# One decoder layer on one core: norm factors per token in partitions, both residual steps on VectorE through PSUM, and a tail in groups of chunks

## The reference

```python
x = x + 0.5 * rmsnorm(swiglu(rmsnorm(x, g1_pre), gate1, up1, down1), g1_post)     # D_FF 5632
p = rmsnorm(x, g_mix_pre) @ w_in              # q k v o | conv a b | input and forget gates
mix = concat[mlstm(q, k, v, gates) * sigmoid(o), silu(layernorm(conv31(a * sigmoid(b))))]
x = x + rmsnorm(mix @ w_out, g_mix_post)
x = x + 0.5 * rmsnorm(swiglu(rmsnorm(x, g2_pre), gate2, up2, down2), g2_post)
# rmsnorm(x, g) = x * rsqrt(mean(x*x) + 1e-6) * g
```

## Time and profile before

| what | us |
|---|---|
| median of three runs (lowest, highest) | 2255.87 (2255.12, 2260.18) |
| the profiled execution, its own time | 2259.16 |
| span of the profiled execution | 2257.5 |
| TensorE busy | 2202.1 |
| VectorE, ScalarE, GpSimd busy | 1008.4, 893.8, 1097.4 |

### The profile page before, as it was taken

How to read it: one execution, slowest core, us unless ns; L and a number is a source line. 1 busy time by engine, 2 the same in 40 slices (tenths; PEclk the granted TensorE clock), 3 DMA queues, 4 the chain that set the end, 5 groups by cost and what they waited for, 6 DMA issues and landing times. The chain is left out here.

```text
span 2257.5 us, 42395 instructions
## 1 busy us (share of the span) xinstructions
PE 2202.1 (98%) x16454; PEld 2183.2 (97%) x16454; DVE 1008.4 (45%) x1329; ACT 893.8 (40%) x1138; POOL 1097.4 (49%) x635
## 2 busy tenths in 40 slices
PE   8999999999999998999999998999999999999995
PEld 8999999999999998899999998999999999999995
DVE  7533332233333227867757716633332223334324
ACT  5433333333333334444344535433333333333331
POOL 4444443344444446656657576444444334444444
PEclk9999999999999999999999999999999999999998
DMA  5545555545545543445645453445445445454452
GB/s 213 163 164 166 166 168 166 163 157 167 167 164 165 169 163 117 165 171 195 219 162 205 150 177 117 150 167 165 163 161 171 165 161 168 164 163 158 168 166 88
DMA packets 100312, 371.20 MB, mean 164 GB/s; under 512 B 11120, under 2 KB 13296, under 8 KB 99216
## 3 DMA queue, kind: packets, MB, share of 16 engines
q1 hardware_dynamic: 96192, 349.93, 46.6%
q10 hardware_dynamic: 3920, 20.18, 2.5%
q0 software_dynamic: 128, 0.07, 0.0%
HBM read 357.06 MB, written 13.07 MB: 164 GB/s over the span
## 5 line engine op out<-in xcount | busy, mean ns | idle before, releaser
L1466 POOL TENSOR_TENSOR wlo<-raw,whi 128x1024 fp32r<-128x1024 f32 x369 | 892.8, 2421 | 827.9 <-ACT whi L736 816.2
L382 PE MATMUL bank<-xh,whi 128*128 128x288 f32 x3600 | 1079.3, 300 | 19.8 <-DVE xl L1040 19.6
L383 PE MATMUL bank<-xl,whi 128*128 128x288 f32 x3600 | 1066.2, 296 | 0.0
L384 PE MATMUL bank<-xh,wlo 128*128 128x288 f32 x3600 | 1065.7, 296 | 0.0
L736 ACT ACTIVATE whi<-raw 128x1024 fp32r<-128x1024 f32 x658 | 694.5, 1057 | 654.5 <-PE bank L384 639.2
L1023 DVE TENSOR_TENSOR wlo<-raw,whi 128x1024 fp32r<-128x1024 f32 x289 | 419.5, 1452 | 757.1 <-ACT whi L736 757.0
L382 PEld LDWEIGHTS bank<-xh,whi 128*128 128x128 f32 x3600 | 680.5, 189 | 26.9 <-issue 14.1
L383 PEld LDWEIGHTS bank<-xl,whi 128*128 128x128 f32 x3600 | 683.7, 190 | 0.3
L384 PEld LDWEIGHTS bank<-xh,wlo 128*128 128x128 f32 x3600 | 680.5, 189 | 0.0
L384 PE MATMUL bank<-hh,wlo 128*128 128x288 f32 x1408 | 417.5, 296 | 0.0
L382 PE MATMUL bank<-hh,whi 128*128 128x288 f32 x1408 | 416.1, 296 | 0.0
(11 more groups left out here) (211 smaller groups left out, 1197.8 us busy)
## 6 DMA issues: line engine op xcount, KB each, us to landing
raw<-stream SPq DMA_DIRECT2D x658, 512.0 KB, 3.4
C<-c_in ACTq DMA_DIRECT2D x4, 2048.0 KB, 8.5
cs_out<-C ACTq DMA_DIRECT2D x4, 2048.0 KB, 8.9
x_res<-x_in SPq DMA_DIRECT2D x4, 576.0 KB, 9.4
y_out<-x_res SPq DMA_DIRECT2D x3, 576.0 KB, 2.8
conv_out<-upad ACTq DMA_DIRECT2D x4, 302.0 KB, 6.8
...
```

Of the source, the lines that this page charges most:

```text
L382: pe.matmul(out, wh, mov_hi[:, k, :], start=first, stop=False)
L383: pe.matmul(out, wh, mov_lo[:, k, :], start=False, stop=False)
L384: return pe.matmul(out, wl, mov_hi[:, k, :], start=False, stop=last)
L1466: pool.tensor_tensor(wlo[:, g % SLOTS, :], raw[:, g % SLOTS, :], whi[:, g % SLOTS, :].bitcast(F32), ALU.subtract).then_inc(lo_ready[g % SL ...
```

## The change

Sums of squares are now made with 128 tokens in partitions: three one-column products with the data as the stationary side (`token_sums`), so the factor takes steps on 128 x 3 values; it is spread back to a row over all partitions by TensorE into PSUM bank 4 (`norm_row_to`). GpSimd no longer adds the last square of a post-norm; TensorE sums `ssq` and that square into one bank (`post_norm`). For pre-norms ScalarE copies the row to `rstd`. In `residual` VectorE takes over GpSimd's product, writes it to PSUM bank 6 or 7 and adds it to x from there; it also makes the lower halves of pieces 4 to 9 there, all six. ScalarE loads the root's table ahead of the last square. In the tail ScalarE has scaled y by the gain, and VectorE does chunks 0 to 11 in four groups, GpSimd chunks 12 to 15 in two. The last loops that this touches are written out.

```diff
-NEXT_LOW = {4: 6, 5: 9, 6: 10, 7: 13, 8: 14, 9: 16}
+NEXT_LOW = {4: 6, 5: 8, 6: 10, 7: 12, 8: 14, 9: 16}
+LAST_GROUPS = ((0, 4), (4, 8), (8, 10), (10, 12))
+LAST_POOL = ((12, 14), (14, 16))
+BLOCKS = (0, P, TOK - P)
 FIRST = 4
...
 
-def dve_splits(g):
...
         return g - HEAD_P - LOOK in DVE_LO
+    if i is None and (GATE_P + 4 <= g <= GATE_P + 9 or FFN2_P + 4 <= g <= FFN2_P + 9):
+        return True
...
-        bank = [ctx.enter_context(nc.psum_tensor(f"bank{i}", [P, 512], F32)) for i in range(8)]
+        psum = ctx.enter_context(nc.psum_tensor("bank", [P, 8, 512], F32))
+        bank = [psum[:, i, :] for i in range(8)]
...
-            groups = ((0, 4), (4, 8), (8, 12), (12, 14), (14, 16))
-            for a, b in groups:
-                sp.wait_ge(x_new, 2 * XC + b)
+            for n, (a, b) in enumerate(LAST_GROUPS):
+                sp.wait_ge(y_new, n + 1)
                 sp.dma_start(y_out[:, a:b, :], x[:, a:b, :]).then_inc(out_stored, 16)
-            sp.wait_ge(out_stored, 16 * len(groups))
+                if 0 < n <= len(LAST_POOL):
+                    c, d = LAST_POOL[n - 1]
+                    sp.wait_ge(y_pool, n)
+                    sp.dma_start(y_out[:, c:d, :], x[:, c:d, :]).then_inc(out_stored, 16)
...
 
-            def column_sums(out, src):
-
-                pe.matmul(out, ones[:, :], src, start=True, stop=True).then_inc(norm_sum, 1)
+            def token_sums(src, first, last):
+
+                for c, lo in enumerate(BLOCKS):
+                    mm = pe.matmul(bank[7][:, c:c + 1], src[:, lo:lo + P], ones[:, 0:1], start=first and c == 0,
+                                   stop=last, skip_group_check=True)
+                if last:
+                    mm.then_inc(norm_sum, 1)
+
+            def norm_row_to(k, banks):
+
+                pe.wait_ge(norm_fac, k + 1)
+                for b in banks:
+                    for c, (lo, n) in enumerate(((0, P), (P, P), (2 * P, NS))):
+                        mm = pe.matmul(bank[b][:, lo:lo + n], nfac[:, c:c + 1].broadcast_to([P, P]),
+                                       ident[:, P - n:P], start=True, stop=True)
+                    mm.then_inc(norm_row, 1)
+
+            def post_norm(stage, k, banks, idle):
+
+                pe.wait_ge(ssq_added, SQ_BUFS + (XC - 1) * (stage + 1))
+                token_sums(ssq, True, False)
+                keep_warm(idle)
+                pe.wait_ge(sq_ready, XC * (stage + 1))
+                token_sums(sq[:, 1, :], False, True)
+                keep_warm(idle)
+                norm_row_to(k, banks)
 
             def down(T, g, per_tile, tiles, n_chunks, tper, gper, i, h_from):
...
                         def square_sum(k):
-                            if k == CH - 1:
+                            if k == 10:
                                 pe.wait_ge(xsq_sum, sums)
-                                column_sums(bank[4][:, 0:TOK], y[:, 0, :])
+                                token_sums(y[:, 0, :], True, True)
+                            if k == XC - 1:
...
 
+            post_norm(0, 1, (4,), 4)
             keep_warm(8)
-            pe.wait_ge(ssq_added, SQ_BUFS + XC)
-            column_sums(bank[4][:, 0:TOK], ssq[:, :])
-            keep_warm(20)
-
...
+                if (p, j) == (MIX_FROM + 1, 2):
                     pe.wait_ge(xsq_sum, 2)
-                    column_sums(bank[4][:, 0:TOK], y[:, 0, :])
+                    token_sums(y[:, 0, :], True, True)
+                if (p, j) == (MIX_FROM + 1, CH - 1):
+                    norm_row_to(2, (4,))
                 if (p, j) == (88, 5):
...
+            post_norm(1, 3, (4,), 4)
             keep_warm(8)
-            pe.wait_ge(ssq_added, SQ_BUFS + 2 * XC)
-            column_sums(bank[4][:, 0:TOK], ssq[:, :])
-            keep_warm(20)
             ffn(FFN2_P, FFN2_T, sum(FF_HALVES), 2 * XC, 3)
 
-            pe.wait_ge(ssq_added, SQ_BUFS + 3 * XC)
-            column_sums(bank[4][:, 0:TOK], ssq[:, :])
...
 
+            def sqrt_table(k):
+
+                act.activation(warm[:, k:k + 1], ones[:, 0:1], ACT.Sqrt)
+
             def norm_root(k, scale):
 
-                act.activation(warm[:, k:k + 1], ones[:, 0:1], ACT.Sqrt)
                 act.wait_ge(norm_var, k + 1)
-                act.activation(scr[:, 6, :], scr[:, 5, :], ACT.Sqrt, scale=scale).then_inc(norm_sd, 1)
+                act.activation(nsd[:, 0:3], nvar[:, 0:3], ACT.Sqrt, scale=scale).then_inc(norm_sd, 1)
+
+            def copy_rstd(k, rows):
+
+                act.wait_ge(norm_row, rows)
+                act.activation(rstd[:, :], bank[4][:, 0:TOK], ACT.Copy).then_inc(rstd_ready, 1)
 
...
+                        sqrt_table(norm_at)
                         norm_root(norm_at, 1.0)
+                        copy_rstd(norm_at, norm_at + 1)
...
 
-                            act.wait_ge(tile_evicted, at(T + t + 1, tiles, i))
-                            act.wait_ge(ssq_added, at(SQ_BUFS + sq_from + t - 1, tiles, i))
-                            act.activation(sq[:, (sq_from + t) % 2, :], y[:, at(d0 + t, tiles, i), :],
-                                           ACT.Square).then_inc(sq_ready, 1)
+                            c = d0 + t
+                            if c == XC - 1:
+                                sqrt_table(norm_at)
+                            act.wait_ge(tile_evicted, T + t + 1)
+                            act.wait_ge(ssq_added, SQ_BUFS + sq_from + c - 1)
+                            act.activation(sq[:, c % 2, :], y[:, c, :], ACT.Square).then_inc(sq_ready, 1)
+                            if norm_at == 5:
+                                act.activation(y[:, c, :], y[:, c, :], ACT.Copy, scale=gain("g_ffn2_post", c))\
+                                   .then_inc(y_scaled, 1)
                         t += 1
...
             act.wait_ge(vec_landed, 16)
             x_operands(0, "g_ffn1_pre", None, START_SPLITS)
             ffn(0, 0, 0, 0, 0)
+            norm_root(1, 4.0)
             split_hi(GATE_P + 3)
-            norm_root(1, 4.0)
             x_operands(GATE_P, "g_mix_pre", 0, NEXT_SPLITS)
             split_hi(GATE_P + 10)
...
-                n = XC + t
-                act.wait_ge(ssq_added, at(SQ_BUFS + n - 1, 4, i))
+                act.wait_ge(ssq_added, at(SQ_BUFS + XC - 1 + t - 1, 4, i))
                 if first:
                     act.wait_ge(mix_ready, 2 * H)
-                act.activation(sq[:, n % 2, :], y[:, at(t, 4, i), :], ACT.Square).then_inc(sq_ready, 1)
+                act.activation(sq[:, t % 2, :], y[:, at(t, 4, i), :], ACT.Square).then_inc(sq_ready, 1)
 
             for t in range(4):
                 out_squares(t, True, None)
-            with act.Fori(1, XC // 4) as i:
+            with act.Fori(1, XC // 4 - 1) as i:
...
+            for p in range(8):
+                split_hi(OUT_P + p + LOOK, 8, XC // 4 - 1)
+                if p == 7:
+                    sqrt_table(3)
+                if p >= 4:
+                    out_squares(p - 4, False, XC // 4 - 1)
+            norm_root(3, 1.0)
             split_hi(FFN2_P + 3)
...
+            ffn(FFN2_P, FFN2_T, sum(FF_HALVES), 2 * (XC - 1), 4)
             norm_root(5, 4.0)
+            act.wait_ge(norm_row, 7)
+            act.activation(rpost[:, :], bank[5][:, 0:TOK], ACT.Copy).then_inc(rpost_ready, 1)
 
...
 
-            def norm_factor(k, out):
+            def norm_factor(k):
 
                 dve.wait_ge(norm_sum, k + 1)
-                dve.tensor_scalar(scr[:, 5, :], bank[4][:, 0:TOK], 1.0 / D_MODEL, EPS, ALU.mult, ALU.add)\
+                dve.tensor_scalar(nvar[:, 0:3], bank[7][:, 0:3], 1.0 / D_MODEL, EPS, ALU.mult, ALU.add)\
                    .then_inc(norm_var, 1)
                 dve.wait_ge(norm_sd, k + 1)
-                ins = dve.reciprocal(out[:, :], scr[:, 6, :])
-                if out is rpost:
-                    ins.then_inc(rpost_ready, 1)
-                else:
-                    link(ins)
+                dve.reciprocal(nfac[:, 0:3], nsd[:, 0:3]).then_inc(norm_fac, 1)
 
             def x_lo(pre, c, n_x):
...
-
+            def residual(g, k, post, pre, n_x, n_new):
+
+                dve.wait_ge(norm_row, k + 1)
                 for c in range(XC + 1):
                     if c < XC:
                         for p in NEXT_LOW:
                             if NEXT_LOW[p] == c:
                                 split_lo(g + p)
+                        t = bank[6 + c % 2][:, 0:TOK]
+                        if c > 1:
+                            dve.wait_ge(x_new, n_new + c - 1)
+                        dve.scalar_tensor_tensor(out=t, in0=y[:, c, :], scalar=gain(post, c), in1=bank[4][:, 0:TOK],
+                                                 op0=ALU.mult, op1=ALU.mult).then_inc(t_ready, 1)
                         dve.wait_ge(t_ready, n_new + c + 1)
-                        dve.scalar_tensor_tensor(out=x[:, c, :], in0=scr[:, c % 4, :], scalar=gain(post, c),
```

(88 more changed lines are left out.)

71 lines of the change are left out of this document (31 added, 40 removed).

## The result

The kernel after takes **2226.2 us** (median of 4 runs, 2225.92 to 2226.61), the kernel before 2257.98 on the same chip in the same rounds (median of 4). The ratio is 0.986, with a 95% interval of 0.9843 to 0.9877: 31.8 us faster. The forecast was 2235.2 with a range of 2229 to 2243. The span went from 2257.5 to 2224.4 us, by 33.1.

What follows compares the result with a forecast made beforehand. TensorE's weight pieces bound the kernel almost everywhere, so only its waits at two residual junctions and the tail could pay; 7.2 + 6.3 - 1.0 + 8.2 = 20.7 us off 2255.87 gave 2235.2 us, range 2229 to 2243.

Steps and rivals of the forecast that it cites:

- the sum: Whole kernel: gains at first junction 7.2, second 6.3 and tail 8.2, less first norm 1.0, make 20.7 us.
- VectorE's gate operations behind `rstd` stay as they were: Head stage after junction 1: VectorE's gate chain, which TensorE waits for, is unchanged, so the 7.2 us gain is kept.
- `rstd` used, gain at junction 1: FFN 1 to the gate tile: `rstd` serves at 903.8 instead of 910.95, gain 7.2 us, bounds 4.5 to 9.6.
- junction 2, less the late table: w_out to FFN 2: `rstd` 7.2 us earlier, less 0.9 for the sigmoid's table load after it, gain 6.3 us.
- first norm, loss: First norm: tree unchanged, sums and row cancel the shorter wait, late table load costs 1.0 us (0 to 2).
- tail, gain: After the last eviction: the tail takes 15.5 us instead of 23.7, gain 8.2 us, bounds 6 and 10.
- PSUM for the residual's product: Residual loop: product into PSUM 0.51 plus 0.03 us, add from it 0.43, PSUM reads no dearer than SBUF; chunk 1.40.
- GpSimd gets into the tree: Second norm: GpSimd's split of piece 11 holds up the tree's other three steps until 897.3; tree done 899.6.
- The new wait brings the clock down: Rival at the junctions: TensorE's 2.1 us wait at k = 10 drops its clock, half the gain goes, 2241; chance 0.18.
- Only the tail pays: Rival: residual chunks need 1.85 us, `rstd` comes no earlier at the junctions, 2250 us is left; chance 0.05.
- slower than before: Rival: semaphores hold each product into PSUM and add from it; at 1.04 us each, 2272 us; chance 0.04.
- The rule on the port: VectorE operations with two SBUF inputs and GpSimd operations shut each other out; those with at most one do not.

Runs made afterwards that it cites:

- a1: The kernel before with the three small tiles added and unused, which moves xl by 96 bytes; 2246.92 us against 2257.18, ratio 0.9953.
- a2: The kernel after with its three small tiles at the end of the memory, xl back at its old address; 2235.78 us, ratio 0.9902 to before.
- b1: The kernel after with the residual's product written to an SBUF buffer instead of PSUM; 2230.68 us against 2259.02 for before, ratio 0.9877.
- b4: The kernel after with piece 11's lower half on VectorE, earlier sums and row, ScalarE's split and table load before the row, first head tiles likewise; 2215.06 us.
- d2: The kernel after with only piece 11's lower half made by VectorE behind the factor instead of GpSimd ahead of it; 2223.88 us, ratio 0.9844 to before.
- b5: The kernel after without the warm-up products of both junctions; 2230.63 us, ratio 0.9877 to before.

## Why the prediction was right and wrong

**The step that failed** is the sum: 7.2 + 6.3 - 1.0 + 8.2, with nothing for the stages between. It costs the new tiles at nothing, without naming them, and takes a product at "about 0.132 us" where gate and up products of the kernel before ran at 0.1333. The missing term is some 11 us by the marks. `a1` shows it alone (10.3 us with nothing but three unused tiles) and `a2` shows the rest without it (2235.8 against 2235.2 forecast; 9.6 us more than after). The new tiles' `sb(...)` lines came with the change, and the trace of before has the two paces: down products at 132.2 and gate products at 133.3 ns, of one shape and one clock. That tells neither the cause nor the sign, but such a difference over 10,800 products is 12 us, more than the whole width of the forecast's own bounds.

**A second step failed and was hidden**: that VectorE's gate operations behind `rstd` stay as they were, so that the head passes the first junction's gain on. From `rstd`'s first use to the last of the decay rows (ScalarE, L834 before, L884 after) it was 22.8 us before, and is 24.8 in after and 25.1 in `a2`; the one gate step of 0.63 us that became 2.60 accounts for it in after. In `a2`, where the products run at before's pace, the head (from `rstd`'s use to the last eviction of w_out) took 462.3 us, and before 459.8: **2.5 us lost**, 1.4 in the new wait for an eviction and 1.1 in the longer wait for the rows (3.8 against 2.7). After shows a gain of 2.3 there, by the faster products and by the clock: it is at half for 6.8 us behind the rows where before and `a2` have 10.2, and it doesn't fall at about 1215, where those two have 3.4 us at half behind an equal wait of 2.3 us.

That `a2` comes within 0.6 us of the forecast is therefore partly luck. Against the forecast it lost these 2.5 us and won 1.2 at the first norm (reached at 54.53, no loss), 0.8 at each junction, and its tail was right within 0.1.

Point by point, times counted from the last eviction's start:

| step | forecast | measured |
|---|---|---|
| row of the factor ready for VectorE | 4.1 | 3.6 (859.35) |
| first product | 6.95 | 6.24 |
| a chunk on VectorE | 1.40 | 1.35 |
| end of `project_first`, gain | 9.7 | 9.3 |
| tree with GpSimd's piece in it | to 7.2 | 7.31 |
| TensorE's wait at the sums | 2.1 | 1.0 |
| `rstd` used, gain at junction 1 | 7.2 | 8.0 |
| junction 2, less the late table | 7.2 - 0.9 | 7.7 - 0.6 |
| first norm, loss | 1.0 | 1.3 in after, none in `a2` |
| head, loss in `a2` | 0 | 2.5 |
| tail, gain | 8.2 | 8.3 |

- *PSUM for the residual's product:* right. The add from PSUM takes 0.46, the product into it 0.52. `b1`'s add from SBUF takes the same 0.46 while GpSimd is quiet, and 1.95 beside it. The Trainium skill (VectorE: DVE Perf Modes, section on the TRN2 errata) would have the reads of PSUM dearer; these rows show no such cost. What the step saves is one collision a junction, which costs 4.5 us for the two junctions together, with the clock behind it.
- *GpSimd gets into the tree:* right, 7.31 us against 5.23 in `b4` and `d2`, where its piece is taken away. The rival that it stays out didn't hold.
- *The new wait brings the clock down* (the rival of junctions that give back half): it didn't; the wait was 1.0 us. `b5` shows what the warm-up is worth, 4.4 us.
- *Only the tail pays* and *slower than before:* no. Both asked for chunks of 1.85 us and more.
- *The rule on the port*, as the prediction puts it ("one with at most one SBUF input does not"), is too wide: the gate step at 900.80 has one SBUF tensor as input (with one scalar for each partition) and took 2.60 us beside GpSimd's splits, against 0.36 in `b4` without them. For the residual's two operations it held: four of them took 0.46 to 0.52 us beside the split of piece 3 (from 859.19).

What stays open is how an address sets the pace. Shown is that tiles moved by 32 or 96 bytes, with no change in any instruction's kind or order, move it by 1.1 ns in 133, and that stages at the same address can still differ by 2.2.
